# The norm's root and reciprocal on four numbers per partition instead of 512

## The reference

```python
def rmsnorm(x, g):
    xf = x.astype(jnp.float32)
    y = xf * lax.rsqrt(jnp.mean(xf * xf, axis=-1, keepdims=True) + EPS)
    return (y * g.astype(jnp.float32)).astype(x.dtype)

def modulate(x, norm_g, ada):
    shift, scale, gate = jnp.split(ada, 3, axis=-1)
    return rmsnorm(x, norm_g) * (1 + scale) + shift, gate
...
    h, gate = modulate(x, norm_g, (c_act @ w_ada + b_ada)[:, None, :])
    hc, gate_c = modulate(xc, norm_g, cc_act @ w_ada + b_ada)
    u = h @ w_in
```

## Time and profile before

| | us |
|---|---|
| median of 3 runs | 1322.59 |
| lowest, highest | 1319.38, 1323.63 |
| the profiled execution, its time | 1322.9 |
| its span in the trace | 1321.1 |
| PE busy | 1258.6 |
| DVE busy | 733.7 |
| ACT busy | 534.6 |

### The profile page before, as it was taken

The page is one execution under the profiler, slowest core; times in us unless marked ns, Lnnn a source line. Parts: engine busy times, 40 slices in busy tenths (PEclk is TensorE's granted clock), DMA queues, the critical chain, the costliest instruction groups (busy, mean ns, idle before and its releaser), DMA issues.

```text
span 1321.1 us, 17033 instructions
## 1 busy us (share of the span) xinstructions
PE 1258.6 (95%) x7004; PEld 970.9 (73%) x7004; DVE 733.7 (56%) x1188; ACT 534.6 (40%) x843; POOL 8.2 (1%) x10
## 2 busy tenths in 40 slices
PE   3798999999999999999999999989999999999996
PEld 1465777767777777776777777758887998889995
DVE  3443436687565555552343233385789976755554
ACT  5222344452223334453332122244665554565452
POOL 0000100000000000000000000000000000000000
PEclk9999999999999999999999999989999999999998
DMA  9999655446443333333454554453332433325541
GB/s 343 332 320 324 220 201 212 191 192 263 155 187 128 128 127 127 128 128 134 169 225 175 213 208 173 186 191 104 120 131 93 160 128 128 128 96 192 182 169 64
DMA packets 76317, 233.73 MB, mean 177 GB/s; under 512 B 8016, under 2 KB 50128, under 8 KB 54352
## 3 DMA queue, kind: packets, MB, share of 16 engines
q1 hardware_dynamic: 76240, 232.65, 49.0%
HBM read 230.54 MB, written 2.10 MB: 176 GB/s over the span
## 4 chain that ended last, share of the span: by engine, by line
PE 83%; DVE 7%; DMA 5%; ACT 3%; issue 1%; SPq 0%; DVEq 0%; ACTq 0%
PE psum_block L614 21%; PE psum_block L615 20%; PE psum_block L616 20%; PE psum_ada L501 5%; PE psum_scores L691 3%; PE psum_scores L648 2%; PE psum_scores L669 2%; DMA raw<-in_w_ada 2%; DVE w_lo L1077 2%; DMA Y<-in_xT 1%; PE psum_scores L682 1%; DMA qreg<-in_w_ada 1%; DVE T L1128 1%; DVE h_lo L1135 1%; DMA glu<-in_w_ada 1%
## 5 line engine op out<-in xcount | busy, mean ns | idle before, releaser
L614 PE MATMUL psum_block<-h_hi,w_hi 128*128 128x512 f32 (+1 forms) x1616 | 562.4, 348 | 0.7 <-ACT glu L1050 0.7
L615 PE MATMUL psum_block<-h_lo,w_hi 128*128 128x512 f32 (+1 forms) x1616 | 547.9, 339 | 0.0
L616 PE MATMUL psum_block<-h_hi,w_lo 128*128 128x512 f32 (+1 forms) x1616 | 547.7, 339 | 0.0
L1077 DVE TENSOR_TENSOR w_lo<-raw,w_hi 128x1024 fp32r<-128x1024 f32 x218 | 263.4, 1218 | 398.6 <-ACT w_hi L803 398.4
L803 ACT ACTIVATE w_hi<-raw 128x1024 fp32r<-128x1024 f32 x218 | 228.5, 1053 | 530.1 <-PE psum_block L616 516.2
L614 PEld LDWEIGHTS psum_block<-h_hi,w_hi 128*128 128x128 f32 x1616 | 306.3, 190 | 78.1 <-issue 38.7
L615 PEld LDWEIGHTS psum_block<-h_lo,w_hi 128*128 128x128 f32 x1616 | 306.6, 190 | 35.3 <-issue 3.8
L616 PEld LDWEIGHTS psum_block<-h_hi,w_lo 128*128 128x128 f32 x1616 | 306.4, 190 | 34.2
L1276 DVE SCALAR_TENSOR_TENSOR Y<-glu,small,Y 128x512 f32<-128x512 f32 (+1 forms) x240 | 130.4, 612 | 0.0
L501 PE MATMUL psum_ada<-raw,cstat 128*32 128x512 f32 x512 | 67.2, 616 | 5.4 <-DMA raw<-in_w_ada 5.4
L917 ACT ACTIVATE T<-psum_scores,stats 128x512 f32<-128x512 f32 (+1 forms) x48 | 28.9, 615 | 52.7 <-DVE stats L1301 52.7
(11 more groups left out here) (174 smaller groups left out, 1105.6 us busy)
## 6 DMA issues: line engine op xcount, KB each, us to landing
raw<-in_w_blocks SPq DMA_DIRECT2D x105, 1024.0 KB, 4.8
raw<-in_w_ada SPq DMA_DIRECT2D x81, 1024.0 KB, 5.5
qreg<-in_w_ada SPq DMA_DIRECT2D x10, 1024.0 KB, 11.2
glu<-in_w_ada SPq DMA_DIRECT2D x5, 1024.0 KB, 9.7
Y<-in_xT SPq DMA_DIRECT2D x4, 1024.0 KB, 12.4
T<-in_xT SPq DMA_DIRECT2D x16, 256.0 KB, 7.2
raw<-in_w_blocks SPq DMA_DIRECT2D x4, 896.0 KB, 11.4
raw<-in_pw SPq DMA_DIRECT2D x2, 1024.0 KB, 6.2
```

The lines of the kernel that those rows point to most:

```text
L614: mm(ps[:, 0:n], hi, hh[:, k, t], start=(at == 0), stop=False)
L615: mm(ps[:, 0:n], hi, hl[:, k, t], start=False, stop=False)
L616: last = mm(ps[:, 0:n], lo, hh[:, k, t], start=False, stop=(at == DT - 1))
L1077: V.tensor_tensor(wl[:, u % 4, 0:n], raw_of(item)[:, cols], wh[:, u % 4, 0:n].bitcast(F32), ALU.subtract).then_inc(*C.up("lo", u))
```

## The change

For the norms at the head of the two layers, `rms_mm` takes the squares as the stationary operand and one column of ones as the moving one, tile by tile of 128 tokens: the sums land in PSUM as 128x4, with tokens on partitions. ACT takes the root of 128x4 into `stats`, DVE its reciprocal, and DVE multiplies an identity matrix by each of the four columns into `T[:, 7, :]`, four diagonal 128x128 matrices side by side. PE multiplies ones by that (`rms_spread`), which gives each token's value in every partition, and ACT copies the 128x512 result from PSUM to `tbuf`. The norm after the last layer keeps its form. On PE the spread stands one ada product behind the sums. The waits on the bank `psS` in the head of each layer are moved from the root to the copy.

```diff
             def rms_mm(l):
 
-                n = TOK if l < LAYERS else LAT
+                if l < LAYERS:
+                    pe.wait_ge(*C.at("rms_add", l, DT - 2))
+                    pe.wait_ge(*C.at("rms_sq", l, DT - 1))
+                    for t in range(TOK // P):
+                        mm(psS[:, 0, t:t + 1], T[:, 4, t * P:(t + 1) * P], ones[:, 0:1], start=True, stop=False)
+                        last = mm(psS[:, 0, t:t + 1], T[:, 2 + (DT - 1) % 2, t * P:(t + 1) * P], ones[:, 0:1],
+                                  start=False, stop=True)
+                    last.then_inc(*C.up("rms_mm", l))
+                    return
...
+            def rms_spread(l):
+
+                pe.wait_ge(*C.at("rms_diag", l))
+                mm(psS[:, 1, :], ones, T[:, 7, :], start=True, stop=True).then_inc(*C.up("rms_spread", l))
+
...
             rms_mm(0)
-            for item in ada0(0)[2:]:
+            for item in ada0(0)[2:-1]:
                 ada0_mm(*item[1:])
+            rms_spread(0)
+            ada0_mm(*ada0(0)[-1][1:])
             ada0_tp(0)
...
                         rms_mm(l)
-                        for a in PLAN[NB]:
+                        ada_mm(*PLAN[NB][0])
+                        rms_spread(l)
+                        for a in PLAN[NB][1:]:
                             ada_mm(*a)
...
             def rms_std(l):
-                n = TOK if l < LAYERS else LAT
                 act.wait_ge(*C.at("rms_mm", l))
-                fn(tbuf[:, 0:n], psS[:, 0, 0:n], ACT.Sqrt, scale=1.0 / D, bias=eps[:, 0:1]).then_inc(*C.up("rms_std", l))
...
+                fn(st[:, 0, :], psS[:, 0, 0:TOK // P], ACT.Sqrt, scale=1.0 / D, bias=eps[:, 0:1]).then_inc(*C.up("rms_std", l))
+                act.wait_ge(*C.at("rms_spread", l))
+                fn(tbuf[:, :], psS[:, 1, :], ACT.Copy).then_inc(*C.up("rstd", l))
...
             def rstd(l):
...
+                V.reciprocal(st[:, 1, :], st[:, 0, :]).then_inc(*C.up("rms_recip", l))
+                dve.wait_ge(*C.ago("rms_recip"))
+                dve.wait_ge(*C.at("rounded"))
+                V.tensor_tensor(T[:, 7, :].rearrange("p (t c) -> p t c", c=P), ident.unsqueeze(1).to_broadcast([P, TOK // P, P]),
+                                st[:, 1, :].unsqueeze(2).to_broadcast([P, TOK // P, P]), ALU.mult).then_inc(*C.up("rms_diag", l))
+                dve.wait_ge(*C.at("rstd", l))
```

More of the change, by code:

```diff
@@ L554, in mm_chunk @@
                             if k == 0 and b == 2:
-                                pe.wait_ge(*C.at("rms_std", 0))
+                                pe.wait_ge(*C.at("rstd", 0))
                             ps = bank(b)
@@ L580, in mm_quarter @@
                         elif b == 2:
-                            pe.wait_ge(*C.at("rms_std", 1))
+                            pe.wait_ge(*C.at("rstd", 1))
                 for i in range(QT):
@@ L835, in rms_std @@
             def rms_std(l):
-                n = TOK if l < LAYERS else LAT
                 act.wait_ge(*C.at("rms_mm", l))
-                fn(tbuf[:, 0:n], psS[:, 0, 0:n], ACT.Sqrt, scale=1.0 / D, bias=eps[:, 0:1]).then_inc(*C.up("rms_std", l))
+                if l == LAYERS:
+                    fn(tbuf[:, 0:LAT], psS[:, 0, 0:LAT], ACT.Sqrt, scale=1.0 / D, bias=eps[:, 0:1]).then_inc(*C.up("rms_std", l))
+                    return
+                fn(st[:, 0, :], psS[:, 0, 0:TOK // P], ACT.Sqrt, scale=1.0 / D, bias=eps[:, 0:1]).then_inc(*C.up("rms_std", l))
+                act.wait_ge(*C.at("rms_spread", l))
+                fn(tbuf[:, :], psS[:, 1, :], ACT.Copy).then_inc(*C.up("rstd", l))
             def modulate(l, k):
@@ L1138, in rstd @@
             def rstd(l):
-                n = TOK if l < LAYERS else LAT
                 dve.wait_ge(*C.at("rms_std", l))
-                V.reciprocal(tbuf[:, 0:n], tbuf[:, 0:n]).then_inc(*C.up("rstd", l))
-                dve.wait_ge(*C.ago("rstd"))
+                if l == LAYERS:
+                    V.reciprocal(tbuf[:, 0:LAT], tbuf[:, 0:LAT]).then_inc(*C.up("rms_recip", l))
+                    dve.wait_ge(*C.ago("rms_recip"))
+                    return
+                V.reciprocal(st[:, 1, :], st[:, 0, :]).then_inc(*C.up("rms_recip", l))
+                dve.wait_ge(*C.ago("rms_recip"))
+                dve.wait_ge(*C.at("rounded"))
+                V.tensor_tensor(T[:, 7, :].rearrange("p (t c) -> p t c", c=P), ident.unsqueeze(1).to_broadcast([P, TOK // P, P]),
+                                st[:, 1, :].unsqueeze(2).to_broadcast([P, TOK // P, P]), ALU.mult).then_inc(*C.up("rms_diag", l))
+                dve.wait_ge(*C.at("rstd", l))
             def h_chunk(c):
```

1 line of the change is left out of this document (added).

## The result

The changed kernel took 1325.93 us, the median of 16 runs (1322.31 to 1330.25), against 1321.6 for the kernel before in 16 runs beside it (1318.34 to 1327.0). The ratio is 1.0032, 95% interval 1.0019 to 1.0045: 4.2 us slower, between 2.5 and 5.9. The forecast was +3.9 on the profiled execution and 1327.0 for the time; the range 1323 to 1331.5 holds the median. The profiled execution after took 1326.62 us with a span of 1324.8, against 1322.9 and 1321.1 before.

The account below looks back on a forecast made before the run. TensorE, busy 95% of the span, bounds the kernel; the change counts only where it stands still. Opening +1.6 and boundary +2.3 make +3.9 on the profiled 1322.9, 1326.8, said as 1327 us; range 1323 to 1331.5.

Parts of the forecast that it names:

- The opening, mechanism: First norm, chunk 0: ScalarE's spread copy delays two roundings and the ada copy, which VectorE then waits for; +1.6 us.
- S + 3.34: Opening: VectorE can read the transposed ada rows 3.34 us after S, the spread's end; break-even is S = 31.2.
- The opening, size: Opening's term: VectorE's first read at 36.1 instead of 34.55, +1.6 us, bounds -0.3 to +4.3.
- S = 32.8: Opening: predicted end of the spread, which starts at 31.4 behind one ada group and takes 1.4 us.
- My 0.20: Opening: assumed us for each of sixteen one-column passes, 3.2 in all; bounds 0.10 and 0.34 each.
- The boundary: Between the layers: spread behind a load-waiting ada product makes PE wait for VectorE; +2.3 us, bounds +1.3 to +4.0.
- The relay: Opening: VectorE, DMA and PE hand on work through eight chunks, so a shift of the first leg shifts all.
- its line of 0.3%: Whole kernel: smallest difference a measurement can tell from no change, 4.0 us, here 1326.6 us.
- Short passes: Rival, both places: passes cost 0.10 and spreads run at full speed; 1323.9, up to 1325.4 us; chance 0.22.
- Slow all through: Rival, both places: passes near 0.34, slow spread, slow first steps; +6 to +8.3 us; chance 0.13.
- Sooner loads: Rival, boundary: ada loads land earlier, -2.0 us there, 1320.6 with the opening's low bound; chance 0.06, including lookalike scatter.
- Swallowed: Rival, opening: its shift vanishes where a load waits for DMA, not its issue; +2.3 alone, 1325 us; chance 0.07.

Follow-up runs that it names:

- e1: Kernel before with the new norm form in layer 0 only, layer 1 old: 1324.21 us against 1321.81, ratio 1.0014.
- e2: Kernel before with the new norm form in layer 1 only, layer 0 old: 1324.41 us, ratio 1.0019.
- e4: As e1, but ScalarE does chunk 0's two weight roundings ahead of the spread's copy in the opening: 1323.49 us, ratio 1.0014.
- e9: Changed kernel with the boundary's spread right behind the sums and the opening's weight roundings ahead of ScalarE's copy: 1322.70 us against 1320.52, ratio 1.0010.
- e5: Kernel before, old norms, with two extra reciprocals ahead of the real one in the opening: 1329.95 us against 1321.05, ratio 1.0060.
- e7: Kernel before, old norms, with both ada products of the boundary put behind layer 1's first pair of products: 1322.94 us, ratio 1.0010.
- e3: As e2, but with the boundary's spread right behind the sums, ahead of both ada products: 1321.70 us, ratio 1.0002.
- e10: Kernel before with layer 1's norm new, spread right behind the sums, second ada product behind the first pair of products: 1320.63 us against 1322.31, ratio 0.9989.

## Why the prediction was right, and where its steps were off

*What bounds, and where it can count.* Right. e1 and e2 put the whole loss into the two places read from the earlier trace rows.

*The opening, mechanism.* Right: VectorE waits for the transposed ada rows behind ScalarE's ada copy, with all of ScalarE's queue ahead of it, and e4 and e9 show what the queue was worth: 0.7 to 0.9 us. What the prediction doesn't name is the path beside it: the last ada group on PE, behind the spread, ended at 35.29, 0.85 us before the ada copy began. Without the queue the opening would have lost some 2 us all the same. The path behind the spread was S + 3.34 and measured 37.12 - 33.95 = 3.17.

*The opening, size.* The term was +1.6 and measured +2.7. The sum was S = 32.8, from sums that start at 26.57; it came out at 33.95 from sums that start at 26.51. Three prices were low. The spread was taken at 1.4, the middle between 1.92 and 1.05, and took 2.02 on the chain: +0.62. The ada group ahead of it was taken over from the row of before, 1.62, and took 1.86: +0.24. The sixteen passes were taken at 0.20 each and took 3.56 in all: +0.36. The path after it was 0.17 shorter. All three took what these forms take at the lower clock: the spread 2.08 in the timeline, as at the boundary, where the windows show 0.50. The windows of the opening read 1.00 there (see the last section), so that the clock is the cause is read from the durations and not shown. It is not the load on the DMAs: the kernel before moved 347 to 349 GB/s in 26 to 34 us, while its passes were slow and while they were fast. The step that was off is the choice of the middle: I let the speed double 5 us after PE began, as in the row of before. By the duration of the ada groups it doubled near 31.6 us before (a mix of 1.93 and 1.04 that makes 1.62) and near 34.7 in the changed kernel (1.43, at 33.86), and in none of the five executions with the new opening was the group ahead of the spread fast; it took 1.93 in all of them. In the seven with the old one it took 1.07 to 1.94 at that place. The point at which the speed comes back scatters from one execution to the next with the old form too. That the new form moves it later is likely from these twelve, but not shown. Either way the price of a step near this point belongs to the slow side.

*The price of the one-column passes.* My 0.20 stood between two rows. In the opening a pair took 0.43, so 0.21 a pass; at the boundary 859.05, 859.29, 859.52 and so on give 0.22 to 0.24 a pair, 0.11 a pass. The page's rule that I weighed (the Trainium skill, TensorE: Matmul & The Clock Gate, LDWEIGHTS: 107 ns for 128 columns) fits the boundary, where the engine was at full speed. In the opening, at half speed by its durations, twice that was paid, and the rival that rested on 0.10 there is out.

*The boundary.* +2.3 against +2.64 in the profiled execution and in e2, 22.24, the same as in the change, 22.18. Each step came as written, counted from the ada groups no more than 0.3 us later: the spread behind the waiting product, at half speed, 2.08 instead of 1.92; the copy 0.60 and the modulation at once; the first product with VectorE as its releaser; the `h_lo` pairs 1.71 apart (872.16, 873.87, 875.58). What I could not foresee from one trace is that the old form scatters as well: 19.54 and 19.35 in the kernel before and e1, 20.44 and 20.79 in e4 and e5. Against all four the new form loses between 1.4 and 2.9. That scatter is in how long PE's first products stay slow. The first product itself hardly varies: it comes 13.06 to 13.23 us behind the ada groups in all six executions in which PE waits for both loads, and 15.98 and 16.01 us behind them with the full spread between the two ada products.

*The relay.* The prediction says that a shift of its first leg shifts all of it. e5 shows this for 6.7 us, within 1.5. The profiled execution has the last chunk only 1.0 us later than before, at 150.01 instead of 149.00, but the relay varies by 6.7 us between executions (110.64 to 117.26), so that this says nothing by itself. The five relays with the new form average 112.6 us, the seven with the old one 114.1; the difference would fit a part won back, and is no larger than their scatter allows.

*The sum.* The terms read from the traces make +5.3, the time says +4.2 (2.5 to 5.9). That my +3.9 came so near the time is luck: the two terms together were 1.4 too small, most of it in the opening, and the time came out 1.1 below what the traces of the two places add up to. Whether the rest is scatter or a part of the opening's 2.7 that is won back stays open; e1 (+0.3 to +3.3) allows both. The measured 0.32% also lies where the prediction drew its line of 0.3% between slower and same, to which it gave 0.50 and 0.46: the case was rightly called close.

*The rivals.* Short passes: at the boundary the passes were short and it changed nothing, in the opening they were not. Slow all through: half of it came true, the spreads were slow, PE's first products after the boundary were fast. Sooner loads: the first came at 865.96, and e7, which takes the loads away and gains nothing, shows that this would have uncovered the norm. Swallowed: out as a whole by e5, which leaves room for 1.5 us of it.

## What to carry to other kernels

A shorter operation on an engine that nobody waits for gains nothing, and one that is waited for by 0.8 us, as in this opening, gains 0.8 at most; when it is bought by new hops across in-order engines, price each hop's place: what stands ahead of it on its engine, and what has been waiting behind it without harm until now. Here a 3.35 us reciprocal was replaced by a 0.18 one and 3.4 us of diagonal, spread and copy, so that even with the spread straight behind the sums (e3) the new form only broke even. Put the short dependent step ahead of work that waits for a DMA, not behind it, and take the slow price for everything near the point where TensorE's speed comes back.

## What the runs showed that I had not expected

- The same spread behind the same 1.36 us of idle PE took 2.08 us in e3 and 2.07 in e10, but 1.20 in e9. In all three the sums ahead of it ran at full speed. In that order, the granted clock read 0.77, 0.63 and 1.00 during the stop, and 0.50, 0.50 and 0.85 under the spread. A stop of this length can cost the higher clock, or not; what decides it stays open.
- The clock that the windows show and the durations don't agree in the opening. The changed kernel's window of 26 to 30 us reads 1.00 while a pair of passes takes 0.43 us, against 0.22 to 0.24 at the boundary; only 38 to 41 us reads 0.51. I went by the durations there; which of the two is right is not shown.

```profile
26.00:30.00 4.00, 3.49 (x17) 3.49 (x17) 0.44 (x1) 1.65 (x2) 0.00 (x0) 1.00 1.10 349
...
38.00:41.00 3.00, 2.69 (x28) 1.19 (x20) 2.96 (x7) 0.98 (x3) 0.00 (x0) 0.51 1.04 332
```

- The relay of eight chunks takes between 110.6 and 117.3 us from one execution to the next, whatever the norm's form. Runs of one kernel differ by 8 us here, and this relay alone varies by 6.7; a single trace can't settle a question of 2 us across it.
